# Weight tiles interleaved in pairs, and the operand buffers moved 128 bytes, in an fp32 two-block transformer kernel

## What is computed

```python
x = x + g2[:, None, :] * squared_relu_mlp(h, w_up[i], w_down[i])   # layers 0 and 1
z = h @ w_in[l] + b_in[l]
y_b = (hb * jax.nn.gelu(z_rg, approximate=True)) @ lru_w_out[l]
x = x + (jax.nn.silu(h @ ffn_w1[l]) * (h @ ffn_w3[l])) @ ffn_w2[l]
```

## Time and profile before

| | us |
|---|---|
| median of 2 runs | 1012.83 (1012.66 to 1013.0) |
| the profiled execution, its own time | 1013.9 |
| its span, first to last instruction | 1012.1 |
| TensorE busy with matmuls | 977.0 |
| TensorE busy with weight loads | 910.6 |
| VectorE busy | 788.2 |
| ScalarE busy | 560.6 |
| DMA | 222 MB, 219 GB/s over the span |

### The profile page before, as it was taken

One profiled execution on the slowest core, in us unless ns is written; L12 is line 12 of the kernel. 1 busy time (PEld: TensorE's weight loads), 2 busy tenths in 40 slices (PEclk: granted clock), 3 DMA queues, 4 the chain that ended last, 5 costly groups with the idle time before them and its releaser, 6 DMA issues.

```text
span 1012.1 us, 19319 instructions
## 1 busy us (share of the span) xinstructions
PE 977.0 (97%) x7468; PEld 910.6 (90%) x7468; DVE 788.2 (78%) x1370; ACT 560.6 (55%) x922; POOL 105.1 (10%) x134
## 2 busy tenths in 40 slices
PE   4799999999999999999999999999999999999996
PEld 2479998888989899999888999998889999999996
DVE  4757986999777677667876899999998887777554
ACT  3248675444655567776544666677126564444352
POOL 0000000000000000000000000999910000000000
PEclk8799999999999999999999999999999999999998
DMA  9998798887564865554555455453446555555531
GB/s 378 421 419 336 275 378 300 318 325 280 144 203 115 307 239 177 189 186 167 208 179 213 164 193 170 164 208 127 165 139 221 182 187 189 194 179 190 193 116 42
DMA packets 35880, 222.27 MB, mean 220 GB/s; under 512 B 3883, under 2 KB 9180, under 8 KB 9436
## 3 DMA queue, kind: packets, MB, share of 16 engines
q1 hardware_dynamic: 35804, 221.22, 60.6%
HBM read 220.13 MB, written 1.07 MB: 219 GB/s over the span
## 4 chain that ended last, share of the span: by engine, by line
PE 81%; DVE 8%; DMA 4%; ACT 4%; issue 2%; DVEq 0%; SPq 0%; ACTq 0%
PE bank L656 22%; PE bank L645 17%; PE bank L646 16%; PE bank L650 12%; PE bank L982 5%; PE bank L1035 3%; DMA mod_raw<-w_mod 2%; DVE w_lo L1472 2%; PE s_banks L679 1%; ACT w_hi L1109 1%; DVE s_banks L1879 1%; DVE bank L1854 1%; PE s_banks L1035 1%; DMA raw<-weights 1%; DVE ab L1847 1%
## 5 line engine op out<-in xcount | busy, mean ns | idle before, releaser
L1472 DVE TENSOR_TENSOR w_lo<-raw,w_hi 128x1024 fp32r<-128x1024 f32 x284 | 346.3, 1225 | 32.1 <-ACT w_hi L1109 29.7
L1109 ACT ACTIVATE w_hi<-raw 128x1024 fp32r<-128x1024 f32 x284 | 296.1, 1050 | 93.6 <-PE bank L656 89.9
L645 PE MATMUL bank<-xg_hi,w_hi 128*128 128x258 f32 (+1 forms) x1376 | 340.9, 285 | 0.8 <-ACT w_hi L1109 0.5
L646 PE MATMUL bank<-xg_lo,w_hi 128*128 128x258 f32 (+1 forms) x1376 | 336.5, 281 | 0.0
L645 PEld LDWEIGHTS bank<-xg_hi,w_hi 128*128 128x128 f32 x1376 | 259.7, 189 | 5.8 <-issue 4.7
L646 PEld LDWEIGHTS bank<-xg_lo,w_hi 128*128 128x128 f32 x1376 | 260.1, 189 | 0.2
L656 PE MATMUL bank<-xg_hi,w_lo 128*128 128x258 f32 (+1 forms) x1376 | 198.3, 282 | 0.3 <-DVE w_lo L1472 0.3
L656 PEld LDWEIGHTS bank<-xg_hi,w_lo 128*128 128x128 f32 x1376 | 178.5, 189 | 0.8 <-DVE w_lo L1472 0.5
L650 PE MATMUL bank<-hid,w_hi 128*128 128x512 f32 x512 | 127.7, 391 | 0.0
L650 PEld LDWEIGHTS bank<-hid,w_hi 128*128 128x128 f32 x512 | 91.5, 188 | 15.8
L656 PEld LDWEIGHTS bank<-hid,w_lo 128*128 128x128 f32 x512 | 68.5, 188 | 5.3
(11 more groups left out here) (245 smaller groups left out, 1262.0 us busy)
## 6 DMA issues: line engine op xcount, KB each, us to landing
raw<-weights SPq DMA_DIRECT2D x157, 1024.0 KB, 4.9
mod_raw<-w_mod SPq DMA_DIRECT2D x28, 1024.0 KB, 11.4
mod_raw<-w_dots SPq DMA_DIRECT2D x20, 1024.0 KB, 9.6
toep<-bias_by_distance SPq DMA_DIRECT2D x8, 256.0 KB, 5.4
x<-x_in SPq DMA_DIRECT2D x1, 1024.0 KB, 4.9
toep<-bias_by_distance SPq DMA_DIRECT2D x8, 128.0 KB, 3.9
y_out<-yout SPq DMA_DIRECT2D x4, 256.0 KB, 2.4
c_all<-c_row SPq DMA_DIRECT2D x1, 512.0 KB, 14.8
```

What stands on the lines that cost most here:

```text
L645: pe.matmul(dst, hi, r_hi, start=start, stop=False, skip_group_check=True)
L646: pe.matmul(dst, hi, r_lo, start=False, stop=False, skip_group_check=True)
L1109: act.activation(pool_w_hi[:, at, :] if name == "pool" and at < 2 else w_hi[:, at % HL, :], raw[:, slot, (at % 2) * UT * P:(at % 2 + 1) * ...
L1472: ve.tensor_tensor(lo, raw[:, slot, (at % 2) * UT * P:(at % 2 + 1) * UT * P], hi.bitcast(F32), ALU.subtract).then_inc(lo_done, 1)
```

## The change

It does three things. The host writes the tiles of a unit in pairs, element by element: element `n` of tile `2q` and element `n` of tile `2q+1` lie side by side, so a tile is now every second fp32 over 1024 bytes, where it was 512 contiguous bytes. Every matmul that reads a weight tile from `w_hi`, `w_lo`, the pool's split weights or `raw` takes its stationary operand through the new `tile`, with a step of 8 bytes. And 128 bytes of nothing lie behind `w_lo`, so `x` and all buffers behind it start 128 bytes later; `raw`, `w_hi` and `w_lo` stay. Modulo 256 bytes, `hid` and `f` then start at 64, `o` and `act` at 192, and `xg_hi` and `xg_lo` have changed places. Loads, splits, waits and the number of instructions are as they were.

```diff
         w_lo = sb("w_lo", [P, HL, UT * P], F32R)
+        sb("line_behind_w", [P, 2 * HALF])
         x = sb("x", [P, DC, SEQ])
...
+        def tile(unit, s):
+            two = unit[:, (s // 2) * 2 * P:(s // 2 + 1) * 2 * P].rearrange("p (n h) -> p n h", h=2)
+            return two[:, :, s % 2]
...
-                hi = w[0][:, slot, s * P:(s + 1) * P]
+                hi = tile(w[0][:, slot, :], s)
...
-                pe.matmul(bank.rearrange("p (a n) -> p a n", a=2), w_hi[:, slot, s * P:(s + 1) * P], both, start=start, stop=False,
+                pe.matmul(bank.rearrange("p (a n) -> p a n", a=2), tile(w_hi[:, slot, :], s), both, start=start, stop=False,
...
-                lo = w[1][:, slot, s * P:(s + 1) * P]
+                lo = tile(w[1][:, slot, :], s)
...
-                    mm = pe.matmul(out_bank(name, v)[:, 0:SEQ], raw[:, slot, ((at % 2) * UT + k) * P:((at % 2) * UT + k + 1) * P],
+                    mm = pe.matmul(out_bank(name, v)[:, 0:SEQ], tile(raw[:, slot, (at % 2) * UT * P:(at % 2 + 1) * UT * P], k),
...
-        block = np.zeros((P, UT, P), np.float32)
+        block = np.zeros((P, UT // 2, P, 2), np.float32)
         for s, t in enumerate(tiles):
-            block[:, s, :] = t
+            block[:, s // 2, :, s % 2] = t
```

More of the change, by code:

```diff
@@ L1034, in lru @@
                         pe.wait_ge(*freed("lru", m))
-                    mm = pe.matmul(out_bank("lru", m)[:, 0:SEQ], raw[:, slot, ((at % 2) * UT + s) * P:((at % 2) * UT + s + 1) * P],
+                    mm = pe.matmul(out_bank("lru", m)[:, 0:SEQ], tile(raw[:, slot, (at % 2) * UT * P:(at % 2 + 1) * UT * P], s),
                                    rt[:, k, :], start=k == 0, stop=k == RC - 1, skip_group_check=True)
```

## The result

The changed kernel takes 1028.26 us (1027.42 to 1029.11, 2 runs) against 1012.83 before: a ratio of 1.0152, 95% interval 1.0109 to 1.0196. It is slower by 15.4 us, or 1.5%, where 976 was forecast, with a range of 955 to 1072. The profiled execution took 1029.1 us with a span of 1027.3.

The account below looks back on a forecast made before the run. TensorE's matmuls were taken as the bound. Savings of 43.8 us, less 3.2 (up0), 1.6 (558 to 680 us) and 1.9 (native units), made 37.1, from 1013.9 to 976.8, about 975.7 as a median; stated as 976, range 955 to 1072.

Parts of the forecast that it names:

- TensorE bounds the kernel, and the steady stages are matmuls by time from start to start: Long steady stages: TensorE is busy 97% of the span and the chain holds only matmuls, 117.5 ns each in ffn.
- Without loss 256 columns would take about 109 ns: All fp32r matmuls of 256 columns: estimate of about 109 ns, so mix loses 4.3 ns and ffn 8.5.
- one step is left everywhere: Rival, fp32r matmuls: each keeps one loss of about 4.3 ns, 256 columns as in mix; 26 us saved, 987 us; chance 0.12.
- The load itself: I take nothing, as 8 bytes are near to contiguous: Every strided weight load: no added cost taken, between bounds of nothing and some 215 ns a load.
- The two streams then advance side by side and can't cross: Weight load and moving operand of fp32r matmuls: equal paces leave at most one step, 111 ns for 256 columns; 43.8 us saved.
- Native units lose one step, 1.9 us: 28 native units, 448 records: paces become unequal, each record loses 4.3 ns, 1.9 us in all.
- The 128 bytes win and lose nothing: Starts of `act`, `o`, `f`, `hid`: gains of 2.3 and 1.1 us against losses of 1.5 and about 0.8, nothing net.
- twice the turns: Rival, all fp32r matmuls: the strided load needs twice the fetches, losses double by 57.4 us, 1071 us; chance 0.22.
- The load halves its pace: Rival, 5804 narrow matmuls: from about 118 to 215 ns, 560 us more, near 1570 us; chance 0.04.
- The addresses don't matter: Rival, weight loads: their addresses don't cause the losses, which remain; 1013 us, up to 2 us either way; chance 0.20.
- starts over 120: Sign against the forecast: matmul starts in ffn over 120 ns apart would point to the load taking twice as many turns.
- loads longer than 0.19 us: Sign against the forecast: weight loads longer than 0.19 us would point to the load's pace.

Follow-up runs that it names:

- the bench: Separate kernel running only matmuls on constant buffers, over weight steps, widths and starts; at full clock 64 columns took 113 ns with step 1, 118 with step 2.
- every entry: Matmul-only kernel, same buffers entered 12 times after 0 to 11 odd-length matmuls; step 1: ten at 113.3 ns, two at 117.8; step 2: all 120 ns.

## Why the prediction was wrong

- *TensorE bounds the kernel, and the steady stages are matmuls by time from start to start*: right, and the 15 us were found in those times. The counts of matmuls were right too.
- *Without loss 256 columns would take about 109 ns*: wrong. It was drawn from the moving side alone, by halving a native record. The load has a pace of its own, and with step 1 it is 112 to 113 ns, in the bench with 64 or 32 moving columns. So the 113.3 ns of mix held hardly anything to win; only what lay above it could be won, and the case "one step is left everywhere" (987) was the most that could be hoped for. No run came near it: the lowest median is 1010.12 us, and 258 columns never took less than 120 ns.
- *The load itself: I take nothing, as 8 bytes are near to contiguous*: this is the step that failed. The load with step 2 takes 118 ns by itself, 5 more than with step 1, and with 256 moving columns the matmuls come every 120 to 122 ns. The bounds had been drawn at nothing and 215 ns a load; between ends so far apart the sum was made with the lower one, although the fastest narrow matmuls stood at the load's own pace, where any price shows at once. 5804 narrow matmuls are what such a choice is multiplied by.
- *The two streams then advance side by side and can't cross*: no run showed a gain from equal paces. With step 2 every start and every entry gave 120 to 122 ns, where 109 to 113 were forecast. The prediction took the two rates of equal matmuls for a matter of their place; it is half of one, as the same place gave both. Whether crossings are what makes 113 into 118 with step 1 stays open; what is shown is that the place of the moving rows decides whether the lower rate can come, that a run then keeps one of the two, and that the load with step 2 shuts out the lower one.
- *Native units lose one step, 1.9 us*: wrong, 216 ns in both kernels and in the one with them alone. Their load has twice the time.
- *The 128 bytes win and lose nothing*: nearly. Alone they cost 3.6 us, 1.9 of it in the wide matmuls, which had been left out of that sum. The rates of mix and w2 changed places as worked out, w2 by luck as the kernel with `f` alone moved shows. Beside the step the times don't tell their effect: 1.0152 with them and 1.0169 without, with intervals that overlap. The traces do, with 1.7 us less in the wide matmuls.
- *The rivals*: "twice the turns" named the right side, starts later than 118 ns in ffn, but its price (57 us) and its place (wide ones too) were wrong, since nothing was doubled. "The load halves its pace" was the right mechanism at the wrong size: that happens at step 4, where the load takes 232 ns, not at step 2. Between it and "nothing" a case was missing in which the load is a few per cent longer. It would have been slower, if by less: with no narrow matmul under 118 ns, mix, `o`, the narrow ones of `hid` and the 256-column stages lose some 4 us by the earlier trace rows. Of the other 11, some 7 are the 2 ns by which 256 columns beside a load of 118 ns come later than that load, and which only the bench showed. The 3.1 in the stages with 258 columns and the 0.7 in the wide matmuls have no such reason: 258 columns already took 120.4 ns, in the bench they took 122 with either step, and in the kernels with all rows at 64 they took 120.9 without the step and 120.1 with it. Their cause stays open. "The addresses don't matter" is refuted by the kernel with interleaving alone, which changes nothing but where the weights lie within a unit and takes 1030.4 us.
- *What would show it wrong*: "starts over 120" and "loads longer than 0.19 us" were both named, and both are in the trace.

## What to carry to other kernels

Where a matmul's moving operand is short, ask first what the weight load's own pace is: 128 fp32 weight columns took 112 to 113 ns here, so 256 moving columns (107 ns at the full clock) are bound by the load at best, and what makes it longer is paid by each matmul, while in plain fp32 the same load was hidden, and at 320 to 512 columns it cost some 5 ns at most. Keep the stationary operand contiguous: step 2 made the load longer by 5%, step 3 by 55% and step 4 by a factor of two. If a disputed cost is multiplied by thousands and stands beside something nearly as long, don't take the lower bound for it; a bench of one kind of instruction, run at the full clock, gives it.

## What was not expected

- The load's price by lines of 16 bytes: 118, 175 and 232 ns for 64, 96 and 128 lines, and 120 ns for 64 lines with half the columns. At step 4 it is the same 233 ns at both clock levels.
- Matmuls of 256 columns with the same instructions and addresses have at least two stable rates, 113.3 and 117.8 ns, and a run stays in the one in which it settled: two entries of twelve were slow to the end of their 64 matmuls. So a change elsewhere can go with another rate in a stage whose own rows keep their start modulo 256: with `xg` moved, mix went from 2.72 to 2.83 us a unit.
- 258 columns cost more than two more columns' time: up1 took 2.90 us a unit with its rows in the good place, against 2.72 for 256 columns in ffn of the same kernel.
- The place of the moving rows turns the effect of the step around at 512 columns: in the down projections the step cost a matmul 4.6 ns with `hid` at 192 and gave back 2.4 ns with `hid` at 64.
- After matmuls of 64 columns back to back the granted clock fell to 1.2 GHz although TensorE never idled, and there steps 1 and 2 took the same 213 ns.
